# Block one's differential attention: the mix of a unit's two maps moved one round later

## The reference

```python
scores = jnp.einsum("bqhrd,bshrd->bhrqs", qi, k).astype(jnp.float32) * scale
dist = jnp.abs((start + jnp.arange(Q_BLOCK))[:, None] - k_pos[None, :]).astype(jnp.float32)
scores = scores - slopes[None, :, None, None, None] * dist[None, None, None]
probs = jax.nn.softmax(scores, axis=-1)
w = probs[:, :, 0] - lam * probs[:, :, 1]
return jnp.einsum("bhqs,bshe->bqhe", w.astype(v.dtype), v)
```

## Time and profile before

| what | us |
|---|---|
| median of 3 runs | 3348.16 |
| lowest and highest | 3346.34, 3350.59 |
| the profiled execution | 3349.58 |
| its span, first to last instruction | 3347.8 |
| TensorE busy in the span | 3084.8 (92%) |
| VectorE busy | 2086.4 (62%) |
| ScalarE busy | 1182.9 (35%) |
| GpSimd busy | 526.5 (16%) |

### The profile page before, as it was taken

One profiled execution on the slowest core, in us unless ns is written; L12 is line 12 of the kernel. 1 busy time (PEld: TensorE's weight loads), 2 busy tenths in 40 slices (PEclk: granted clock), 3 DMA queues, 4 the chain that ended last, 5 costly groups with the idle time before them and its releaser, 6 DMA issues. The chain is left out here.

```text
span 3347.8 us, 38192 instructions
## 1 busy us (share of the span) xinstructions
PE 3084.8 (92%) x14528; PEld 2430.9 (73%) x14528; DVE 2086.4 (62%) x3086; ACT 1182.9 (35%) x2199; POOL 526.5 (16%) x537
## 2 busy tenths in 40 slices
PE   6999999998888879989998878999879999999999
PEld 5787876776777768767887657745557788888887
DVE  6111744787778844848998887789866444444444
ACT  2211331576666742224233767111353211111110
POOL 2000003444111100131244235010001000000000
PEclk9999999999999989999999979999899999999999
DMA  6323125445533334341256160331001111111111
GB/s 229 124 91 108 51 73 190 164 132 149 157 101 101 92 132 142 132 115 32 82 177 195 50 201 22 111 112 55 30 3 60 51 51 51 51 51 51 38 51 63
DMA packets 189728, 324.05 MB, mean 97 GB/s; under 512 B 16418, under 2 KB 111810, under 8 KB 189546
## 3 DMA queue, kind: packets, MB, share of 16 engines
q1 hardware_dynamic: 168682, 248.72, 24.0%
q0 software_dynamic: 20864, 72.89, 6.0%
HBM read 232.14 MB, written 88.11 MB: 96 GB/s over the span
## 5 line engine op out<-in xcount | busy, mean ns | idle before, releaser
L216 PE MATMUL banks<-b3mlpw_part,b3mlp_acthi 128*128 128x512 f32 x1024 | 315.3, 389 | 0.0
L216 PE MATMUL banks<-b3h4a_hi,b3mlpw_part 128*128 128x512 f32 x960 | 301.4, 393 | 2.1 <-DVE b3mlpw_part L3685 2.1
L216 PE MATMUL banks<-b1ln_w,b_hThi 128*128 128x512 f32 x768 | 238.2, 391 | 0.0
L3730 DVE TENSOR_TENSOR b3out_x<-b3out_x,banks 128x1024 f32<-128x1024 f32 x128 | 154.7, 1219 | 111.7 <-PE banks L216 111.7
L216 PEld LDWEIGHTS banks<-b3mlpw_part,b3mlp_acthi 128*128 128x128 f32 x1024 | 192.3, 188 | 40.0
L216 PEld LDWEIGHTS banks<-b3h4a_hi,b3mlpw_part 128*128 128x128 f32 x960 | 180.7, 188 | 43.7 <-DVE b3mlpw_part L3685 2.6
L3701 ACT ACTIVATE b3mlp_relu<-banks 128x1024 f32<-128x1024 f32 x32 | 32.9, 1029 | 495.7 <-PE banks L216 495.7
L510 PE MATMUL banks<-b_hThi,b1item_hi 128*128 128x512 f32 x464 | 196.2, 423 | 3.4 <-DVE b1item_lo L499 3.1
L216 PE MATMUL banks<-b3mlpw_part,b3mlp_actlo 128*128 128x512 f32 x512 | 199.2, 389 | 0.0
L216 PE MATMUL banks<-b3out_lo,b3mlpw_part 128*128 128x512 f32 x480 | 190.6, 397 | 0.0
L3719 DVE TENSOR_TENSOR b3mlp_relu<-b3mlp_relu 128x1024 f32<-128x1024 f32 x32 | 39.2, 1225 | 241.8 <-ACT b3mlp_relu L3701 241.8
(11 more groups left out here) (462 smaller groups left out, 6981.7 us busy)
## 6 DMA issues: line engine op xcount, KB each, us to landing
qk_spill<-b1scan_qk SPq DMA_DIRECT2D x64, 256.0 KB, 3.0
b1att_k<-qk_spill SPq DMA_DIRECT2D x64, 256.0 KB, 7.4
b1out_ws<-in_w_out SPq DMA_DIRECT2D x16, 1024.0 KB, 5.0
b3mlpw_stage<-in_w_mlp_down SPq DMA_DIRECT2D x16, 1024.0 KB, 4.8
b2h_stage<-in_w_in SPq DMA_DIRECT2D x30, 512.0 KB, 4.4
b3mlpw_stage<-in_w_mlp_up SPq DMA_DIRECT2D x15, 1024.0 KB, 5.2
b1item_stage<-in_w_in SPq DMA_DIRECT2D x29, 512.0 KB, 4.9
b1ln_stage<-in_w_in SPq DMA_DIRECT2D x12, 1024.0 KB, 7.7
```

The lines of the kernel that those rows point to most:

```text
L216: last = pe.matmul(out, x, y, start=i == 0, stop=i == n - 1)
L3730: v.tensor_tensor(K.m4.x3[:, st], K.m4.x3[:, st], pair, ALU.add).then_inc(S["ml_acc"], 1)
```

## The change

Mix, turn, copy, value products and all that follows for a unit come one round later: r-2 in place of r-1 for turn and copy, r-3 for r-2 for the value products, r-4 for r-3 for square, mean-square step and output step, r-6 for r-5 for the turn of the output and its copy. VectorE keeps the mix at unit r-1 but does it behind the two minima of unit r and the mean-square step, ahead of the output step. All three loops run one round more. The minima's wait for the mix is for that of two units back. The small steps that are moved are unchanged.

```diff
 def pe_att(K):
-    for r in range(UNITS + 5):
+    for r in range(UNITS + 6):
...
-        u = r - 5
+        u = r - 6
         if u >= 0:
             pe.wait_ge(S["att_y"], u + 1)
             if u + 2 < UNITS:
                 pe.wait_ge(S["att_sq"], u + 3)
             pe.transpose(K.bank[u % 2][:, P:2 * P], m.out[u % 2], K.eye).then_inc(S["att_yt"], 1)
-        u = r - 1
+        u = r - 2
...
             pe.wait_ge(S["att_mix"], u + 1)
             transposed(pe, K.pair[3], ...).then_inc(S["att_turned"], 1)
-        u = r - 2
+        u = r - 3
...
 def act_att(K):
-    for r in range(UNITS + 5):
-        u = r - 3
+    for r in range(UNITS + 6):
+        u = r - 4
...
-        u = r - 5
+        u = r - 6
...
-        u = r - 1
+        u = r - 2
...
 def dve_att(K):
-    for r in range(UNITS + 5):
-        u = r - 1
-        if 0 <= u < UNITS:
-            s, m0, m1 = K.stat[u % 12], m.map0[u % 3], m.map1[u % 2]
-            v.wait_ge(S["att_exp"], 2 * u + 2)
-            vs.mark(v.reciprocal(s[:, 4:5], s[:, 3:4]))
-            then(v.tensor_scalar(s[:, 6:7], s[:, 2:3], s[:, 2:3], LN_EPS, ALU.mult, ALU.mult))
-            then(v.scalar_tensor_tensor(s[:, 5:6], s[:, 4:5], s[:, 2:3], K.lam[:, 2:3], ALU.mult, ALU.mult))
-            v.scalar_tensor_tensor(m0, m1, s[:, 5:6], m0, ALU.mult, ALU.add).then_inc(S["att_mix"], 1)
-        u = r - 3
-        if 0 <= u < UNITS:
-            s = K.stat[u % 12]
-            v.wait_ge(S["att_sq"], u + 1)
-            v.scalar_tensor_tensor(s[:, 8:9], s[:, 7:8], 1.0 / P, s[:, 6:7], ALU.mult, ALU.add).then_inc(S["att_ms"], 1)
+    for r in range(UNITS + 6):
         if r < UNITS:
...
-            if r:
-                v.wait_ge(S["att_mix"], r)
+            if r >= 2:
+                v.wait_ge(S["att_mix"], r - 1)
             if r >= 3:
                 v.wait_ge(S["att_turned"], r - 2)
             for i, mp in enumerate((m.map0[r % 3], m.map1[r % 2])):
                 v.wait_ge(S["att_sc"], 2 * r + i + 1)
                 v.tensor_tensor_reduce(mp, K.pair[1 + i], ...).then_inc(S["att_shift"], 1)
-        u = r - 3
+        u = r - 4
+        if 0 <= u < UNITS:
+            ...
+        u = r - 1
+        if 0 <= u < UNITS:
+            ...
+        u = r - 4
         if 0 <= u < UNITS:
             ...
```

More of the change, by code:

```diff
@@ L1453, in dve_att @@
                 v.tensor_tensor_reduce(mp, K.pair[1 + i], m.dist[:, x0:x0 + S_LEN], -1.0, 3e38, ALU.add, ALU.min, s[:, i:i + 1]).then_inc(S["att_shift"], 1)
-        u = r - 3
+        u = r - 4
+        if 0 <= u < UNITS:
+            s = K.stat[u % 12]
+            v.wait_ge(S["att_sq"], u + 1)
+            v.scalar_tensor_tensor(s[:, 8:9], s[:, 7:8], 1.0 / P, s[:, 6:7], ALU.mult, ALU.add).then_inc(S["att_ms"], 1)
+        u = r - 1
+        if 0 <= u < UNITS:
+            s, m0, m1 = K.stat[u % 12], m.map0[u % 3], m.map1[u % 2]
+            v.wait_ge(S["att_exp"], 2 * u + 2)
+            vs.mark(v.reciprocal(s[:, 4:5], s[:, 3:4]))
+            then(v.tensor_scalar(s[:, 6:7], s[:, 2:3], s[:, 2:3], LN_EPS, ALU.mult, ALU.mult))
+            then(v.scalar_tensor_tensor(s[:, 5:6], s[:, 4:5], s[:, 2:3], K.lam[:, 2:3], ALU.mult, ALU.mult))
+            v.scalar_tensor_tensor(m0, m1, s[:, 5:6], m0, ALU.mult, ALU.add).then_inc(S["att_mix"], 1)
+        u = r - 4
         if 0 <= u < UNITS:
```

## The result

The changed kernel takes 3305.89 us (median of four executions, 3297.50 to 3307.55), the kernel before 3348.70 beside it. The ratio is 0.986, 95% interval 0.9848 to 0.9872: 1.3 to 1.5% faster. The forecast was 3292, the range 3284 to 3313. The execution profiled after is the fastest of the four, 3297.50 with a span of 3295.7; the other three took 3305.52 to 3307.55.

What follows compares the result with a forecast made beforehand. A closed ring of waits between engines, 5.57 us a unit, was taken to bound attention; with TensorE's 4.65 instead, start, units and drain put the last copy 55.8 us earlier, 3348.2 - 55.8 = 3292.4, said as 3292, range 3284 to 3313.

Steps and rivals of the forecast that it cites:

- The ring and what takes its place: Block one's attention: minimum, exponentials, mix, next minimum take 5.57 us a unit; once cut, TensorE's 4.65 binds, VectorE's 4.54 close.
- The head's rescaling: At a head's first unit VectorE rescales distances, 1.15 us; slack covers 0.47, leaving 0.7 us of stall a head.
- Units 54 to 63: Last rounds, with output-projection weight steps on VectorE: VectorE binds at 5.74 in six rounds; 50.0 us in all.
- the 0.8 for round 54: Extra 0.8 us in round 54, where ScalarE's 4.29 + 1.0 was taken as the longest.
- The drain: From unit 63's first minimum to the last copy: 23.7 us against 19.4, so the extra round gives back 4.3.
- Edits at nothing: Moved waits, small steps, load queues, GpSimd's stores and buffers in the attention stage were taken to cost nothing.
- The start: First units of attention: values land at 851.9, unit 4's first minimum at 855.1 in place of 862.2; gain 7.1 us.
- The sum: Whole attention stage: last copy ends at 1165.5 against 1221.27, 55.8 us earlier, so 3348.2 becomes 3292.4.
- the second rival: Attention rounds: thin slack, restarts or ScalarE's square make a round 4.9 to 5.0, +13 to +17, 3307 us; chance 0.14.
- the third rival: TensorE, now the bound, pays for stretches at 1.2 GHz; 20 low rounds of 64 give 3385 us; chance 0.03.

Runs made afterwards that it cites:

- sooner stores: The changed kernel, but GpSimd issues the store of each half of turned outputs two units sooner; 3292.09 us, ratio 0.9822.
- the later rounds alone: The kernel before with turn, copy, value products and all behind them one round later, VectorE's mix still ahead of the minima; 3352.48 us.
- shorter bursts: The changed kernel, but from head 2 on the keys' second copy loads only 256 of 1024 columns; 3302.07 us.
- the later wait for the values: The kernel before, but TensorE waits for the second half of the values only at head 4; 3345.28 us.
- the order alone: The kernel before with VectorE's minima of unit r ahead of the mix of unit r-1, turn, copy and value products in their old rounds; 3590.29 us.
- values apart alone: The changed kernel, stores as they are, but TensorE waits for the second half of the values only at head 4; 3302.17 us, ratio 0.9851.

## Why the prediction was right, and where not

- **The ring and what takes its place.** Right. With both parts of the change a round is TensorE's, 4.62 for 4.65; each part alone leaves a ring, of 5.57 and of 8.3. VectorE stands 0.24 behind, not 0.11: its own work is 4.38 for 4.54. Of that, 0.09 is the end of the output step, which the sum counted (0.35) though the next instruction starts after 0.26, and 0.05 the mean-square step, 0.07 behind the minima for 0.12 ahead of them.
- **The head's rescaling.** Right. A head's eight units took 37.72 with sooner stores (879.08 to 916.80), 0.76 over eight rounds of 4.62; forecast 0.7. TensorE idles 0.56 before the output turn at the head of unit 32, released by the square, as forecast.
- **Units 54 to 63.** 47.9 for 50.0, by the same 0.15 of VectorE a round, and the 0.8 for round 54 wasn't paid.
- **The drain.** Right, 23.6 for 23.7: 4.2 us given back.
- **"Edits at nothing": the stores.** This is the step that failed. The prediction put it as "GpSimd's stores keep their place behind the roots", at nothing. They do, but the roots moved. From the issue to the point where ScalarE is ready for the copy it was 10.9 us for the store shown, and is 6.2. And being a round later than the loads, it lands behind a burst of queries and keys in up to 9.9, before 5.0. Neither alone costs: with the later rounds alone these stores have 10.1 us for 8.2 to 8.8, with shorter bursts 6.2 for 5.2 to 6.0. Together they cost 8.6 us in units 4 to 54 (244.2 against 235.6 with sooner stores), in another pair of executions 10.4 (246.1 against 235.7).
- **The start.** Taken at the values' landing in one execution, 17.1; the runs show 16.8 and 21.8 for the same kernel. In the kernel before it took 24.2 and 24.1, and with the later wait for the values 23.6, so the landing cost nothing there that can be told. It went into the sum as a fixed time, and it should have had a range.
- **The sum.** The forecast gain was 55.8 us, the measured one 42.8, about a quarter less; the time is 14 us over the forecast. No profiled execution stands at the median; the two profiled spans, 3295.7 and 3307.0, are 3.7 and 15.0 above the forecast's 3292.0 (3347.8 - 55.8). Of this the table gives units 4 to 54 7.5 and 8.1, the start -0.3 and 4.7, the time before the stage -1.3 and 3.2, behind it 0 and 1.2, and the last rounds and the drain -2.2 and -2.3. The stores are thus a cause in both, and the rest varies between executions for reasons that stay open.
- **The range.** That 3306 lies inside it owes something to luck. The upper part was put there for the second rival, 3307, a round of 4.9 to 5.0 by thin slack. Rounds are 4.62, so that rival's mechanism did not come, and the time was near its number by another. Likewise the sooner stores' median of 3292 is the forecast's number partly by chance: in their profiled execution the start is 4.6 over its term, and units 4 to 63 are 3.2 and the stretch behind the stage 3.3 under theirs.
- **The clock.** 1.00 in the stage (0.99 before): the third rival has nothing for it there. Only at the start, behind the wait for the values, did an execution show 0.54, for 3.7 us.

## What to carry to other kernels

When steps of a software pipeline are moved and its round gets shorter, every transfer tied to a moved step gets another time to land and other neighbours. Work out for each, in us and not in rounds, from its issue to the step that needs it, and set that against its landing beside the loads that will now run with it. Reordering one engine and shifting the others are one edit: here the one alone cost 238 us and the other gained nothing. And cut a profile at fixed marks before you explain a spread: here about half of it lay outside the stage that was changed, and most of the rest at its start.

## What was not expected of the hardware

A 256 KB store from GpSimd's queue lands in 2.3 us when alone, in 5.0 when it is issued 1.35 us behind the first of a burst of twelve loads of 256 KB, and in up to 9.9 when it is issued behind the last. After 3.5 us of idling TensorE's turn and values ran partly at 1.2 GHz in most rounds of the order alone, which made a round of 8.32 one of 9.94, and wholly at 2.4 GHz in one of six. Why the second half of the values takes 20.1 us to land in one execution and 24.5 in another (values apart alone), and why the stretch behind the stage varies between 2123 and 2133, stays open.
